# Decode attention over a paged key cache: keys turned in 32x32 blocks by VectorE, scores as 32-row by 32-column products

## What is computed

```python
q_lat = einsum('bthe,rhe->bthr', q_nope, w_uk)             # 8 sequences, 4 tokens, 8 heads, 256
s_past = einsum('bthr,bsr->bths', q_lat, lat_past) \
       + einsum('bthe,bse->bths', q_rope, kr_past)         # 2048 cached positions of a sequence
s_new = ...                                                # the 4 new positions, causal
p = softmax(concatenate([s_past, s_new]) * SOFTMAX_SCALE)
o_lat = einsum('bths,bsr->bthr', p_past, lat_past) + einsum('bthu,bur->bthr', p_new, ckv)
```

## Time and profile before

| | |
|---|---|
| median of 3 runs | 1291.05 us |
| the profiled execution | 1290.38 us, of which 1288.6 us is the span from first to last instruction |
| TensorE matmul busy | 1235.8 us, 96% of the span |
| VectorE, ScalarE, GpSimd busy | 52%, 41%, 10% |
| decode loop, from the first maximum to the last | 948.7 to 1018.2 us, 7 sequences |

### The profile page before, as it was taken

The page is one execution under the profiler, slowest core; times in us unless marked ns, Lnnn a source line. Parts: engine busy times, 40 slices in busy tenths (PEclk is TensorE's granted clock), DMA queues, the critical chain, the costliest instruction groups (busy, mean ns, idle before and its releaser), DMA issues.

```text
span 1288.6 us, 23720 instructions
## 1 busy us (share of the span) xinstructions
PE 1235.8 (96%) x9991; PEld 1150.7 (89%) x9991; DVE 667.4 (52%) x986; ACT 526.3 (41%) x721; POOL 129.6 (10%) x124
## 2 busy tenths in 40 slices
PE   5899999999999999999999999988899899999997
PEld 2899999989998999999899999978676589999997
DVE  1644445556675445445545545557544456554453
ACT  1534333343335434334544433453633335554322
POOL 3000001300040000032000002210012040000031
PEclk9999999999999999999999999999989999999998
DMA  9777554467766775355678435574266472444442
GB/s 363 284 292 280 202 212 166 163 228 281 243 251 228 281 276 182 130 177 176 228 285 299 175 131 171 197 288 175 83 246 254 172 262 100 177 162 171 136 157 82
DMA packets 68711, 269.45 MB, mean 209 GB/s; under 512 B 4704, under 2 KB 5152, under 8 KB 54416
## 3 DMA queue, kind: packets, MB, share of 16 engines
q1 hardware_dynamic: 35664, 184.57, 40.0%
q10 hardware_dynamic: 29792, 59.09, 12.5%
q0 software_dynamic: 3168, 24.52, 5.3%
HBM read 266.55 MB, written 1.62 MB: 208 GB/s over the span
## 4 chain that ended last, share of the span: by engine, by line
PE 87%; DVE 5%; DMA 4%; ACT 2%; SPq 1%; issue 1%; ACTq 0%; POOL 0%; DVEq 0%; POOLq 0%
PE bank L1257 24%; PE bank L1258 24%; PE bank L1259 24%; PE bank L1303 4%; PE bank L1529 3%; DMA ada_early<-in_w_ada 1%; PE bank L1542 1%; PE bank L1581 1%; DVE w_lo L810 1%; ACT w_hi L598 1%; PE bank L1457 1%; PE bank L1324 1%; DMA stage<-in_w_ci 1%; PE bank L1461 1%; PE bank L1545 1%
## 5 line engine op out<-in xcount | busy, mean ns | idle before, releaser
L810 DVE TENSOR_TENSOR w_lo<-stage,w_hi 128x2048 fp32r<-128x2048 f32 (+2 forms) x182 | 374.8, 2061 | 300.4 <-ACT w_hi L598 300.0
L1257 PE MATMUL bank<-h_hi,w_hi 128*128 128x288 f32 x1608 | 476.0, 296 | 2.3 <-DVE w_lo L810 1.4
L1259 PE MATMUL bank<-h_hi,w_lo 128*128 128x288 f32 x1608 | 474.7, 295 | 0.0
L1258 PE MATMUL bank<-h_lo,w_hi 128*128 128x288 f32 x1608 | 474.2, 295 | 0.0
L598 ACT CAST w_hi<-stage 128x2048 fp32r<-128x2048 f32 (+2 forms) x182 | 304.1, 1674 | 251.3 <-PE bank L1259 170.2
L1257 PEld LDWEIGHTS bank<-h_hi,w_hi 128*128 128x128 f32 x1608 | 301.6, 188 | 6.9 <-issue 3.7
L1259 PEld LDWEIGHTS bank<-h_hi,w_lo 128*128 128x128 f32 x1608 | 301.5, 187 | 0.0
L1258 PEld LDWEIGHTS bank<-h_lo,w_hi 128*128 128x128 f32 x1608 | 301.5, 187 | 0.0
L1258 PE MATMUL bank<-gu_lo,w_hi 128*128 128x288 f32 x768 | 226.6, 295 | 0.0
L1259 PE MATMUL bank<-gu_hi,w_lo 128*128 128x288 f32 x768 | 226.4, 295 | 0.0
L1257 PE MATMUL bank<-gu_hi,w_hi 128*128 128x288 f32 x768 | 225.3, 293 | 0.0
(11 more groups left out here) (230 smaller groups left out, 980.7 us busy)
## 6 DMA issues: line engine op xcount, KB each, us to landing
stage<-in_w_gu SPq DMA_DIRECT2D x88, 1024.0 KB, 4.9
stage_ada<-in_w_ada ACTq DMA_DIRECT2D x53, 1024.0 KB, 9.3
stage<-in_w_down SPq DMA_DIRECT2D x64, 704.0 KB, 4.0
stage<-in_w_ci SPq DMA_DIRECT2D x16, 768.0 KB, 4.4
stage_ada<-in_w_ada SPq DMA_DIRECT2D x9, 1024.0 KB, 10.6
ada_early<-in_w_ada SPq DMA_DIRECT2D x4, 1024.0 KB, 15.0
stage<-in_w_co SPq DMA_DIRECT2D x4, 1024.0 KB, 7.0
stage<-in_w_wo SPq DMA_DIRECT2D x4, 1024.0 KB, 5.7
```

The lines of the kernel that those rows point to most:

```text
L810: nc.vector.tensor_tensor(w_lo[part][:, 0:cols], stage[st_][:, 0:cols], w_hi[part][:, 0:cols], ALU.subtract).then_inc(lo_ready, 1)
L1257: nc.tensor.matmul(out, hi, x_hi, start=start, stop=False)
L1258: nc.tensor.matmul(out, hi, x_lo, start=False, stop=False)
L1259: return nc.tensor.matmul(out, lo, x_hi, start=False, stop=stop)
```

## The change

1. `turn` leaves TensorE. VectorE turns `lat` and `kr_past` with a transposition that works inside 32x32 blocks, from SBUF to SBUF: five `chunks` for a sequence, each 128 x 1024 elements (two feature blocks of 32, for all 16 groups). Each partition quarter i then holds features on its 32 rows, for the positions that lay on these 32 partitions.
2. `score(b, c)` takes, for a chunk, 32 products of 32 rows by 32 columns by 128 columns: 2 feature blocks, 4 quarters t of the output partitions, 4 row tiles i. Row tile i adds up in its own PSUM bank (`s_past`, banks 0 to 3, one buffer).
3. The queries must stand on each of the four row quarters: 10 products with 0/1 matrices (`spread`) repeat them, and ScalarE copies the result to `q_rep` and `q_rep_rope`, before the loop.
4. In the loop TensorE multiplies the probabilities of b-1 by the latents behind the first two chunks of b. ScalarE copies the transposed probabilities instead of VectorE.
5. The latent queries are made with the queries as the 32-column operand (8 products of 256 columns), copied by ScalarE and transposed (4 transpositions).
6. The prompt's attention pipeline gets a lag of three tiles instead of two (`LAG`), with a fourth `p_exp` buffer.
7. `stage_ada` holds `q_rep` during the loop, so its piece of the adaLN unit is loaded last (`TAIL_ORDER`); 8 products of `ones` (`keep_busy`) stand behind the last scores.

The core of the diff:

```diff
-TURNS = QUARTERS * RT + 2
+BLK = 32
+KEY_BLOCKS = (KVL + ROPE) // BLK
+CHUNKS = KEY_BLOCKS // 2
...
+        chunk = [over(f"chunk{c}", [P, GROUPS, 2, BLK], at) for c, at in enumerate((0, 4096, 16384, 20480))] + \
+            [nc.alloc_sbuf_tensor_at("chunk4", [P, GROUPS, 2, BLK], F32, offset=spare_lo)]
...
+        s_banks = ctx.enter_context(nc.psum_tensor("s_banks", [P, P // BLK, 512], F32))
+        s_past = s_banks[:, :, 0:QG * BLK]
...
-                    for q in range(RING):
+                    for q in TAIL_ORDER:
                         if q == 0:
-                            sp.wait_ge(ada_used, LATENT + 1)
+                            sp.wait_ge(chunk_used, CHUNKS * NSEQ)
...
                 if b >= 3:
                     pool.wait_ge(pv_done, b - 2)
-                pool.wait_ge(turned, TURNS * (b - 1))
+                pool.wait_ge(chunk_ready, CHUNKS * (b - 1))
                 gather(b)
...
+                if j == H:
+                    act.wait_ge(q_tok_psum, 1)
+                    nc.scalar.copy(q_tok[:].rearrange("p a n -> p (a n)"), bank[7][:]).then_inc(q_tok_ready, 1)
...
-            for j in range(2 * H + 3):
-                if 2 <= j < 2 * H + 2:
-                    k = j - 2
+            for j in range(2 * H + LAG + 1):
...
             act.wait_ge(q_lat_ready, 2)
             nc.scalar.copy(ckv_tok[0:TS], bank[7][0:TS, 0:KVL]).then_inc(tok_ready, 1)
 
-            def copy_even(b, turns):
-                for k in turns:
-                    act.wait_ge(turned, TURNS * b + k + 1)
-                    dst = lat_t[k % RT][:, k // RT, :] if k < QUARTERS * RT else kr_t[:, k - QUARTERS * RT, :]
-                    nc.scalar.copy(dst, bank[(TURNS * b + k) % 4][:]).then_inc(even_copied, 1)
-
-            copy_even(0, range(0, TURNS, 2))
...
+                act.wait_ge(pv_done, b + 1)
+                nc.scalar.copy(o_part[:, b, :], bank[7][:, KVL * (b % 2):KVL * (b % 2 + 1)]).then_inc(o_part_ready, 1)
+
             for b in range(NSEQ):
-                if b + 1 < NSEQ:
-                    act.wait_ge(sc_psum, b + 1)
-                    copy_even(b + 1, (0,))
+                if b:
+                    part_out(b - 1)
                 act.wait_ge(max_ready, b + 1)
-                if b:
-                    act.wait_ge(pp_psum, b)
-                nc.scalar.activation(p_past[:], bank[4 + b % 2][:], ACT.Exp, bias=neg_past[:, b:b + 1], scale=SCALE,
+                nc.scalar.activation(p_past[:].rearrange("p (j i n) -> p i j n", j=QG, i=P // BLK),
+                                     s_past.rearrange("p i (j n) -> p i j n", j=QG), ACT.Exp,
+                                     bias=neg_past[:, b:b + 1], scale=SCALE,
                                      accum_out=sum_past[:, b:b + 1]).then_inc(p_past_ready, 1)
                 nc.scalar.activation(p_new[0:QS], s_new[:, b, :], ACT.Exp, bias=neg_past[0:QS, b:b + 1], scale=SCALE,
                                      accum_out=new_sum[:, b:b + 1]).then_inc(p_past_ready, 1)
-                if b + 1 < NSEQ:
-                    copy_even(b + 1, range(2, TURNS, 2))
-                act.wait_ge(pv_done, b + 1)
-                nc.scalar.copy(o_part[:, b, :], bank[7][:, KVL * (b % 2):KVL * (b % 2 + 1)]).then_inc(o_part_ready, 1)
...
-                    dst = lat_t[k % RT][:, k // RT, :] if k < QUARTERS * RT else kr_t[:, k - QUARTERS * RT, :]
-                    nc.vector.tensor_copy(dst, bank[(TURNS * b + k) % 4][:]).then_inc(odd_copied, 1)
+            def turn(b, c):
+
+
+                if c == 0:
+                    dve.wait_ge(lat_in[b % 3], 32 * (b // 3 + 1))
+                if b:
+                    dve.wait_ge(chunk_used, CHUNKS * (b - 1) + c + 1)
+                elif c == CHUNKS - 1:
+                    dve.wait_ge(q_rep_psum, KEY_BLOCKS // 2)
+                keys = lat[b % 3][:, :, 2 * BLK * c:2 * BLK * (c + 1)] if c < CHUNKS - 1 else kr_past[b % 2][:]
+                nc.vector.transpose(chunk[c][:].rearrange("p g k n -> p g (k n)"), keys).then_inc(chunk_ready, 1)
 
             dve.wait_ge(sn_psum, 1)
...
             for b in range(NSEQ):
 
-                dve.wait_ge(sc_psum, b + 1)
-                nc.vector.tensor_reduce(max_now[:], bank[4 + b % 2][:], AX_X, ALU.max).then_inc(max_step, 1)
+                if b + 1 < NSEQ:
+                    turn(b + 1, 0)
+                dve.wait_ge(chunk_used, CHUNKS * (b + 1))
+                nc.vector.tensor_reduce(max_now[:], s_past, AX_XY, ALU.max).then_inc(max_step, 1)
                 dve.wait_ge(max_step, 2 * b + 1)
                 nc.vector.tensor_tensor(max_now[0:QS, :], max_now[0:QS, :], new_max[:, b:b + 1], ALU.max)\
                     .then_inc(max_step, 1)
                 dve.wait_ge(max_step, 2 * b + 2)
                 nc.vector.tensor_scalar(neg_past[:, b:b + 1], max_now[:], -SCALE, None, ALU.mult).then_inc(max_ready, 1)
                 if b + 1 < NSEQ:
-                    copy_odd(b + 1, range(1, TURNS // 2 + 1, 2))
-                dve.wait_ge(pp_psum, b + 1)
-                if b:
-                    dve.wait_ge(pv_done, b)
-                nc.vector.tensor_copy(p_past_t[:].rearrange("p g n -> p (g n)"), bank[4 + b % 2][:]).then_inc(pp_ready, 1)
-                nc.vector.tensor_copy(p_new_t[0:TS], bank[6][0:TS, 0:QS]).then_inc(pp_ready, 1)
-                if b + 1 < NSEQ:
-                    copy_odd(b + 1, range(TURNS // 2 + 2, TURNS, 2))
+                    for c in range(1, CHUNKS):
...
-            for rt in range(RT):
-                for h in range(H):
-                    o = (rt * H + h) * TS
-                    mm = nc.tensor.matmul(bank[7][:, o:o + TS], uk_t[:, h, P * rt:P * (rt + 1)], q_nope[:, h, TP:T],
-                                          start=True, stop=True)
-            mm.then_inc(q_lat_psum, 1)
+            for h in range(H):
+                j, g = divmod(h, C_TILES)
+                mm = nc.tensor.matmul(bank[7][TS * g:TS * (g + 1), KVL * j:KVL * (j + 1)], q_nope[:, h, TP:T],
+                                      uk_t[:, h, :], start=True, stop=True)
+            mm.then_inc(q_tok_psum, 1)
             for j in range(H, H + 2 * (TP // P)):
                 keys_values(j)
+                if j == H + 1:
+                    pe.wait_ge(q_tok_ready, 1)
+                    for rt in range(RT):
+                        for g in range(H // C_TILES):
+                            o = P * (rt * (H // C_TILES) + g)
+                            mm = nc.tensor.transpose(bank[7][:, o:o + P], q_tok[:, g, P * rt:P * (rt + 1)], ident[:])
+                    mm.then_inc(q_lat_psum, 1)
 
...
-            def score(b):
-
-                pe.wait_ge(even_copied, TURNS // 2 * (b + 1))
-                pe.wait_ge(odd_copied, TURNS // 2 * (b + 1))
-                if b >= 2:
-                    pe.wait_ge(pp_ready, 2 * (b - 1))
-                for part in range(RT + 1):
+            def score(b, c):
+
+                pe.wait_ge(chunk_ready, CHUNKS * b + c + 1)
+                for k in range(2):
                     for t in range(QUARTERS):
-                        out = bank[4 + b % 2][QS * t:QS * (t + 1), :]
-                        if part < RT:
-                            mm = nc.tensor.matmul(out, q_lat[:, part, b, :], lat_t[part][:, t, :], start=part == 0,
-                                                  stop=False)
-                        else:
-                            mm = nc.tensor.matmul(out, (q_rs, q_rs_low)[t // 2][:, b, :], kr_t[:, t % 2, :],
-                                                  start=False, stop=True)
-                mm.then_inc(sc_psum, 1)
...
+                        for i in range(P // BLK):
+                            rows = slice(BLK * i, BLK * (i + 1))
+                            if c < CHUNKS - 1:
+                                queries, keys = q_rep[rows, 2 * c + k, b, :], chunk[c][rows, QG * t:QG * (t + 1), k, :]
+                            else:
+                                queries = q_rep_rope[k][rows, b, :]
+                                keys = chunk[c][rows].rearrange("p (g h) k n -> p h g k n", h=2)\
+                                    [:, t // 2, QG * (t % 2):QG * (t % 2 + 1), k, :]
+                            mm = nc.tensor.matmul(s_past[QS * t:QS * (t + 1), i, :], queries, keys,
+                                                  start=c == k == 0, stop=c == CHUNKS - 1 and k == 1)
+                mm.then_inc(chunk_used, 1)
...
+            def turn_past(b):
                 for j in range(QG):
                     nc.tensor.transpose(bank[4 + b % 2][:, P * j:P * (j + 1)], p_past[:, P * j:P * (j + 1)], ident[:])
                 nc.tensor.transpose(bank[6][0:TS, 0:P], p_new[:], ident[:]).then_inc(pp_psum, 1)
...
+            pe.wait_ge(spread_ready, 1)
+            for n in range(KEY_BLOCKS // 2):
+                for half in range(2):
+                    k = 2 * n + half
+                    queries = q_lat[:, k * BLK // P] if k * BLK < KVL else q_rs
```

(49 more changed lines are left out.)

121 lines of the change are left out of this document (54 added, 67 removed).

## The result

The changed kernel takes 1318.24 us (median of 4 runs, 1318.13 to 1319.92), the kernel before in the same comparison 1291.64: a ratio of 1.0214, 95% interval 1.0202 to 1.0227. It is slower by 27 us, where 1283.9 was forecast and the range ended at 1305. The profiled execution took 1318.26 us.

The account below looks back on a forecast made before the run. TensorE, full in the decode loop, was taken as the bound, and the gather as the new loop's pace. Loop −3.7, latent queries −2.0, attention −2.8, head +1.5, end +0.5 sum to −6.5: 1290.4 to 1283.9 us, range 1278 to 1305.

Parts of the forecast that it names:

- The score products: In the decode loop: 64 records a chunk at about 7 ns from start to start, taken as 0.5 us a chunk.
- rival (c): Score products: row tiles queue at 28 ns, 1.8 us a chunk; loss beyond 14 ns a record; about 1322 us, chance 0.12.
- that ring, 5s + 5.4: Serial ring of scores, softmax and latent product in the loop, s being us a chunk: 7.9 us a sequence.
- VectorE's 1.2 us a block: In the loop: a block transposition of 1024 columns goes at a column a cycle, 1.2 us.
- Gather ring 8.85: In the loop: each gather waits for an earlier latent product; 17.7 us per two sequences, 8.85 each, setting the pace.
- The clock: In the loop: TensorE's idle stands lower its clock, costing 0.55 us on an average sequence, making the period 9.4.
- Latent queries −2.0 and attention −2.8: Ahead of the loop: remade latent queries save 2.0 us; a third tile of lag saves 2.8 of 4.0 us waiting.
- Head +1.5: Head of the loop, up to the first maximum: 16.3 us instead of 14.8, so +1.5 us.
- end +0.5: After the loop: three quarters of the adaLN unit instead of two behind the weights' transposition, +0.5 us.
- (a): In the loop: the clock stays full because small products keep TensorE at work; 1280.0 us, chance 0.18.
- (b): In the loop: the clock falls in every sequence, 10.1 us each, no change that can be told; 1288.8 us, chance 0.19.
- (d): VectorE's block transposition in the loop takes two cycles a column, 2.4 us; 1316 us, chance 0.07.

Follow-up runs that it names:

- the inconclusive pair: 256 waits a sequence for a semaphore long reached, traced as 128 instructions, added to the changed kernel and to the one before: 1398.21 and 1397.42 us.
- the run with the fill: Changed kernel plus two products of 512 columns a sequence, into an unread bank, while TensorE waits for the exponentials: 1320.0 us.

## Why the prediction was wrong

The step that failed is "The score products": it sized a chunk by how close 64 matmul records can lie, 7 ns, from one run of four records, and took 0.5 us; measured it is 0.88 us where instructions are at hand and the clock is full, 1.16 us over the loop, and 1.62 us a sequence of waiting for instructions come on top, a term that the prediction didn't have. The first records of a sequence do lie as close as it said (timeline of TensorE; the first view ends behind them):

```profile
994.55 0.39 PE L1562 MATMUL s_banks<-chunk,q_rep 32*32 32x128 f32 x16
...
994.55 1.32 PE L1562 MATMUL s_banks<-chunk,q_rep 32*32 32x128 f32 x77
996.72 0.44 PE L1562 MATMUL s_banks<-chunk,q_rep 32*32 32x128 f32 x23 [0.85 <-issue]
```

(0.39 − 0.292) / 15 is 6.5 ns, 0.292 being the first record's own duration. These are the first records of sixteen products, on sixteen tiles, so the row tiles work side by side, and the mechanism of rival (c) did not occur. But this pace lasts only as long as instructions are queued: over 77 records it is (1.32 − 0.29) / 76 = 13.5 ns, and then TensorE stands. The single starts show more. Behind the first sixteen, products start about 17 ns apart, with 128 columns (441 of the 811 steps under 60 ns at full clock lie at 16 to 18 ns) as with 64 (372 of 560); a product's first record is told from its second by its longer duration. That is a price by product, not by column, and the prediction, which counted 160 products for 12 + 40, priced their columns alone.

At full clock and without a stall, 64 records took a median of 0.88 us, just the pace, 14 ns a record, from which rival (c) said that the loop would lose. With 0.88 the prediction's own sum for that ring, 5s + 5.4, is an estimated 9.8 us, as long as before's 9.93 and close to the 10.2 to 10.3 measured with 256 columns, where a chunk takes 0.86 and nothing waits for a block. So the chunk's size alone takes the gain away; the 3.7 us a sequence beyond before come with the waiting for blocks, 1.62, and with the half clock and smaller stalls around it. The DMA queues of the profile before showed no more than 6 blocks in the loop, so nothing there gave a price for the supply. Halving the columns changed nothing; halving the instructions gave back 23.5 us; doubling them cost 74. The first two together exclude that the loop's time goes by columns; that the waits are for blocks rests on the 64 waits that each end behind a block's landing, and on the idle time that grows with the blocks in the loop (none at 11, 3.6 us at 14, 11.4 at the changed kernel's 19, 49.4 at 37). Not separated: in every run but the inconclusive pair the instructions changed together with the weight loads and matmuls that they are, so a price of these in the array may have a part in the 17 ns.

A smaller fault of the same ring is an overlap: it hid two chunks in the 1.63 us from the transposition of the probabilities to the latent product. The transposition is itself TensorE's work, 0.93 us measured, so even two chunks of 0.5 us don't fit.

The 0.7 us of the latent product (3.02 for 2.34) goes with half clock and waits within; in the two quickest of the seven sequences it took 2.3. Point by point:
- VectorE's 1.2 us a block: right, 1.204.
- The softmax's 2.23: right, 2.27.
- Gather ring 8.85, longest of the three: the size was about right (9.21 with hardly any scores), but it did not decide, because TensorE was later.
- The clock: it falls (0.84), as forecast; its price in the changed kernel is small, 1.7 us of the loop in the run with the fill, since what is gained by it is waited for.
- Latent queries −2.0 and attention −2.8: wrong, together −0.05 in the profile. Both took work off TensorE where VectorE's chain ends last: the first uncovered a wait for `q_rope` (2.0 us in the run with these parts alone, 0.7 in the changed kernel), the second left VectorE's pace of the pipeline as it was.
- Head +1.5, measured +2.2; end +0.5, measured −0.5.
- Rivals (a), (b), (d): no. Rival (c) had the sign and, by 4 us, nearly the time, by a mechanism that isn't there; that it came so near is luck.

Two rules of the Trainium skill bear on this. "TensorE: Matmul & The Clock Gate", section "Wait — 56ns, not 53.3ns?", keeps small matmuls about 25 ns apart; the 6.5 ns above disagree, and so do the 13.5. "Runtime: NRT & Kernel Launch", section "Instruction fetch mechanics", says that instructions arrive in blocks of 16 KiB, 256 to a block, fetched ahead of the engine, and that crossing a block's edge is mostly hidden. The size agrees with the 263 bytes measured for a product's four instructions; the hiding does not hold here, where waits of up to 2.9 us, and in the run with twice the instructions 5.3 us, end behind a block.

Still open: why a block that is needed comes so late (the transfer itself takes about 1 us, and without the later gathers half of the waiting stays), and whether the 17 ns between products is the issue of four instructions or the array's handling of their weight loads. None of the runs that compute all scores beats the kernel before. Products of 256 columns keep the loop free of such waits, but cost 10.2 us a sequence against 9.93, with half of the positions left out of the softmax; with all of them the softmax would have twice as many columns on 64 partitions, which was not tried.

## What to carry to other kernels

When a change trades a few wide products for many narrow ones, count TensorE's instructions for the stage beside its columns: here some 720 a sequence were too many for a loop that was to take 9.4 us, some 400 in 10 us were not. A wait that the profile puts down to "issue" (nothing visible) is to be held against the transfers of instruction blocks, and on VectorE against the gathers, before it is blamed on the array or the clock. And work taken off a full engine ahead of a wait for another engine gives nothing: look at what that engine would be late with next.

## What the runs showed of the hardware that was not expected

- TensorE resumes 1.2 to 1.6 us after an instruction block has landed, in all 64 waits above 0.4 us without a visible cause in the loops of six runs; and in none of these loops does a block start sooner than 3.2 us after the one before it, even when the engine stands.
- An instruction that holds two waits for a semaphore reached long ago costs TensorE 118 ns where it is never idle and 89 ns where some of it is (128 a sequence).
- fp32 products on sixteen 32x32 tiles start 6.5 ns apart from instructions already queued, and about 17 ns apart behind them, with 128 columns and with 64.
